# Products of constants issued ahead of twelve TensorE waits in a three-layer forward pass

## The chip, the cores and the metric

The kernel runs on one core of a Trainium2 chip. A core has TensorE (called PE in the profile; its weight loads are PEld), VectorE (DVE), ScalarE (ACT), GpSimd (POOL) and SyncE (SP), which issues most of the DMAs. The metric is the device time of one execution in microseconds. TensorE's clock has two levels, 1.2 and 2.4 GHz; the profile gives the granted share of the higher one, so 0.50 is 1.2 GHz and 1.00 is 2.4 GHz.

## The reference

All tensors are float32, the batch is 1, the sequence 256, the width 1024. A first block has two layers, a second block one:

```python
h = h + even_mixer(rms_norm(h), ...)      # differential attention + gated recurrence (RG-LRU)
h = h + swiglu(rms_norm(h), ...)          # 1024 -> 2816 -> 1024
h = h + pool_mixer(rms_norm(h), ...)      # means over windows of 2, 4, 8, 16
h = h + moe_swiglu(rms_norm(h), ...)      # 8 experts of 3584, top 2 of 8
h = rms_norm(h)
# second block, modulated by c, with 256 tokens of context
x = h + mod[2] * hybrid_mixer(...)        # gated delta rule and GLA, both directions
x = x + mod[5] * hier_moe(...)            # 4 groups of 8 experts of 512, top 2 in a group
out = rms_norm(x)
```

## The kernel before

The program is written engine by engine, each engine with its own list of instructions, and all order between engines is made by semaphores. TensorE's list is the block that begins at L655. `mm` is the matmul call, `chain` a row of calls that add up in one bank, `take(name)` a wait until a block of weights has landed in one of the six slots of the ring. PSUM is one tensor `ps` of eight banks of 512 columns. `table` holds constants: the unit matrix `ident` in columns 0 to 127, then a matrix of ones, a lower and an upper triangle up to column 511.

In order of time TensorE's list is this. The first mixer: projections, `scores`, `gates`, `weights_turned` (transposes of the attention weights, L1000), `weighted`, with the vectors of modulation `ada(0..2)` between them; the output projection; `norm_T(1)` (16 transposes of the normed rows, L693), which waits for them with `xn_ready`. The feed-forward part: 22 chunks, each with 16 gate and up products of 256 columns (L665) and four down products of 512 columns (L1071). `norm_T(2)`, the pooling products, `norm_T(3)`, the router. Then `routed_units`, 56 units of three weight blocks each (products at L782 and L797), which ends in a branch on the number of rounds (L934: the round for overflowing experts is skipped). Then the second block: keys, values and queries of the context and the sequence, the squares of keys (L1129) and of queries (`query_squares`, L1172), the delta rule in ticks (`gram`, `turn`, `product`, `step` and so on, L1219 and L1229 among them), the GLA part with two directions `d` (L1365 transposes, then the state sum, then eight levels of L1388 and L1393), the branch outputs, `norm_T(5, 6)`, the second router (L1459), and `routed_pairs`: ranks (L910), a gather, and 16 pairs of experts (L873, L893, L860).

At each place where TensorE needs something from DVE or ACT there is a `pe.wait_ge`, and the instructions behind it in the list stand still until it holds. The norm of a result is a chain of POOL, DVE and ACT steps, as is the softmax, so TensorE is idle at these places. SP issues each load of weights when the slot is free, that is when TensorE has read the block that was there before: in `routed_units` at L528, for the second block at L520, in `routed_pairs` at L616.

Of the kernel before, what the change touches and what calls it, by code (L numbers as in the profile page):

```python
# [140 lines left out]
def build(nc, ins, out):  # L141

    ctx = ExitStack()
    with ctx:
# [18 lines left out]
        def inc(name):  # L163

            if name not in shared:
                return sem(name)
            k = emitted[name] = emitted.get(name, 0) + 1
            group, value = place[name, k]
            emitted[group] = emitted.get(group, 0) + 1
            assert emitted[group] == value, (name, k)  # L170
            return sem(group)

        def at(name, value):

            if name not in shared:
                return sem(name), value
            group, total = place[name, value]
            return sem(group), total
# [7 lines left out]
        table = sb("table", [P, N_CONST])  # L186
# [8 lines left out]
        ps = ctx.enter_context(nc.psum_tensor("ps", [P, 8, 512], F32))  # L195
# [35 lines left out]
        ident = table[:, C_ID:C_ID + P]  # L231
# [421 lines left out]
        def _(pe):  # L653
            mm = nc.tensor.matmul

            def take(name):
                i = number[name]
                _, src, k, n, _ = entry(i)
                pe.wait_ge(*at("loaded%d" % (i % NSLOT), 16 * (i // NSLOT + 1)))
                return slot(i, k, n)  # L660

            def chain(outp, pairs):
# [2 lines left out]
                    last = mm(outp, l, r, start=(i == 0), stop=(i == n - 1))  # L665
                return last

            def ada(g):

                if g == 0:  # L670
                    pe.wait_ge(*at("c_silu", 1))
                    pe.wait_ge(*at("qk_copied", 2))
                else:
                    pe.wait_ge(*at("rg_sig", g))
                w = [take("ada%d" % (4 * g + j)) for j in range(4)]
                for k in range(KC):
                    for j in range(4):
                        last = mm(ps[32 * j:32 * j + 32, 5 + g % 2, :], scT[k // 4][:, k % 4, :], w[j][:, k, :],
                                  start=(k == 0), stop=(k == KC - 1))
                last.then_inc(inc("ada"), 1)  # L680
# [14 lines left out]
            def norm_T(i, x_at=None):  # L695
                for t in range(NT):
                    for c in range(KC):
                        if c % 4 == 0:
                            pe.wait_ge(*at("xn_ready", 4 * (i if x_at is None else x_at) + 2 * t + c // 4 + 1))
                        last = nc.tensor.transpose(ps[:, c // 2, (c % 2) * S + t * P:(c % 2) * S + (t + 1) * P],  # L700
                                                   xn[:, t, c * P:(c + 1) * P], ident)
                        if t == NT - 1 and c % 2:
                            last.then_inc(inc("xnT_ready"), 1)
# [201 lines left out]
                scatter(PAIRS, 0)  # L905

            def routed_pairs():
                pe.wait_ge(*at("sel2_ready", 1))
                E = E2
                mm(ps[:, 7, 0:E], tri_le, seli[:, 0, 0:E], start=True, stop=True)  # L910
                chain(ps[:, 7, E:2 * E], [(ones, seli[:, 0, 0:E]), (tri_le, seli[:, 1, 0:E])])
                chain(ps[:, 7, 2 * E:3 * E], [(ones, seli[:, 0, 0:E]), (ones, seli[:, 1, 0:E])]).then_inc(inc("rank2_sum"), 1)
                pe.wait_ge(*at("m2_zeroed", 1))
                pe.sem_inc(sem("m2_y"), 2)
                pairs_round("m", 0)
                pe.wait_ge(*at("rounds2_ready", 1))
                rounds = pe.value_load(rounds_i[1][0:1, 0:1], min_val=1, max_val=8)
                with pe.If(rounds > 1):
                    with pe.Fori(1, rounds) as r:
                        pairs_round("x", r)  # L920
# [66 lines left out]
            def gates(g):  # L987

                if g == 0:
                    pe.wait_ge(*at("xb_copied", 1))  # L990
                    pe.wait_ge(*at("xc_ready", 1))
                    pe.wait_ge(*at("wgate_in", 16 * 16))
                else:
                    pe.wait_ge(*at("gb_copied", 1))
                b = 6 - 2 * g
                for m in range(4):
                    last = mm(ps[:, b + m // 2, (m % 2) * S:(m % 2 + 1) * S], wgate[:, g, m, :], xc[:, m, :], start=True, stop=True)
                last.then_inc(inc("gates_ready"), 1)

            def weights_turned(qt):  # L1000
                pe.wait_ge(*at("w_ready", qt + 1))
                for kb in range(qt + 1):
                    for h in range(H):
                        last = nc.tensor.transpose(ps[:, kb, h * P:(h + 1) * P], wts[:, h, kb * P:(kb + 1) * P], ident)
                last.then_inc(inc("wT_ready"), 1)

            def weighted(qt):
                pe.wait_ge(*at("wT_copied", qt + 1))
                for h in range(H):
                    last = chain(ps[:, 2, h * P:(h + 1) * P],  # L1010
                                 [(wT[:, kb, h, :], vtok[:, kb, h * P:(h + 1) * P]) for kb in range(qt + 1)])
                last.then_inc(inc("o_ready"), 1)
# [26 lines left out]
            ada(1)  # L1039
            ada_cols(0)  # L1040
            gates(1)
            weights_turned(1)
            weighted(1)
            ada_cols(1)
            ada(2)
# [4 lines left out]
            for n in range(2):  # L1050
# [3 lines left out]
                    last = chain(ps[:, 4 + 2 * n + t, :], [(mixT[:, k, t * P:(t + 1) * P], w[:, k, :]) for k in range(KC)])  # L1054
                last.then_inc(inc("y_ready"), 1)

            norm_T(1)
            chunks = [(u, j) for u, (f0, n) in enumerate(FU) for j in range(n // P)]
            for n in range(len(chunks) + 1):
# [13 lines left out]
                    last.then_inc(inc("down_done"), 1)  # L1073

            norm_T(2)
            pe.wait_ge(*at("xn_ready", 16))
            pe.wait_ge(*at("hTc_ready", 1))
            pe.wait_ge(*at("hTc_act", 1))
# [25 lines left out]
            for k in range(KC):  # L1104
                piece(2, k)
                for t in range(NT):
                    last = mm(ps[:, 5, t * E1:(t + 1) * E1], hTx[:, k, t * P:(t + 1) * P], rw1[:, k, :],
                              start=(k == 0 and t == 0), stop=(k == KC - 1), skip_group_check=True)
# [2 lines left out]
            routed_units()  # L1111

            w = take("k")
            pe.wait_ge(*at("res_ready", 4))
            for m in range(4):
                chain(ps[:, 4 + m, S:2 * S], [(w[:, k, m * P:(m + 1) * P], hT[:, k, S:2 * S]) for k in range(KC)])
# [5 lines left out]
            for m in range(4):  # L1122
                chain(ps[:, m, 0:S], [(w[:, k, m * P:(m + 1) * P], hTx[:, k, :]) for k in range(KC)])\
                    .then_inc(inc("v2_proj"), 1)
                if m == 1:
                    pe.wait_ge(*at("kraw", 1))
                    pe.wait_ge(*at("k_sq", 1))
                    for h in range(H):
                        last = mm(ps[:, 4 + h, :], ones, sq[:, h, :], start=True, stop=True)  # L1129
                    last.then_inc(inc("k_ss"), 1)  # L1130
# [36 lines left out]

            def query_squares():
                pe.wait_ge(*at("vTok_ready", 1))
                pe.wait_ge(*at("q_sq", 1))  # L1170
                for i in range(2):
                    last = mm(ps[:, 4 + i, :], ones, sq[:, 2 * i:2 * i + 2, 0:S], start=True, stop=True)  # L1172
                last.then_inc(inc("q_ss"), 1)
# [5 lines left out]
            def gram(s_, d):  # L1179
                n, t = 2 * s_ + d, TILE[d][s_]  # L1180
                bx, by = banks(s_, d)
                if s_ >= 2:
                    pe.wait_ge(*at("S_ready", n - 3))
                elif s_ == 1:
                    pe.wait_ge(*at("qF_ready", 1))
                for h in range(H):
                    kf = kF[:, h, t * P:(t + 1) * P]
                    mm(bx[:, h, :], kf, kf, start=True, stop=True)
                for h in range(H):
                    last = mm(by[:, h, :], gdec[:, t, 4 * d + h:4 * d + h + 1].to_broadcast([P, P]), (tri_le, tri_ge)[d],  # L1190
                              start=True, stop=True)
                last.then_inc(inc("gram"), 1)
# [135 lines left out]
            for d in range(2):  # L1328
# [20 lines left out]
                else:  # L1349
# [8 lines left out]
                    last.then_inc(inc("gate_proj"), 1)  # L1358
                    pe.wait_ge(*at("z_silu", 2))

                pe.wait_ge(*at("kd_ready", d + 1))
                pe.wait_ge(*at("hv_ready", 1))
                for t in range(NT):
                    for h in range(H):
                        last = nc.tensor.transpose(ps[:, t, h * P:(h + 1) * P], Wd[:, h, t * P:(t + 1) * P], ident)  # L1365
                last.then_inc(inc("kdT_ready"), 1)
                pe.wait_ge(*at("kdTok_ready", d + 1))
                if d == 1:
                    pe.wait_ge(*at("gate_kept", 2))
# [5 lines left out]
                for l in range(8):  # L1375
                    b = 4 + 2 * (l % 2)
                    n = 8 * d + l
# [8 lines left out]
                    for t in range(NT):  # L1386
                        for h in range(H):
                            last = mm(ps[:, b + t, h * P:(h + 1) * P], kx[:, h, t * P:(t + 1) * P], qx[:, h, t * P:(t + 1) * P],  # L1388
                                      start=True, stop=True)
                    last.then_inc(inc("att_ready"), 1)  # L1390
                    m = l // 2
                    for k in range(4 * (l % 2), 4 * (l % 2) + 4):
                        last = mm(ps[:, m // 2, (m % 2) * S:(m % 2 + 1) * S], w[:, k, m * P:(m + 1) * P], hTx[:, k, :],  # L1393
                                  start=(k == 0), stop=(k == KC - 1))
# [4 lines left out]
                for h in range(H):  # L1399
                    last = mm(ps[:, 3, h * P:(h + 1) * P], kW2[1][:, h, kt * P:(kt + 1) * P], qW2[1][:, h, qt * P:(qt + 1) * P],  # L1400
                              start=True, stop=True)
# [48 lines left out]
                    last.then_inc(inc("grow_sum"), 1)  # L1450

            pe.wait_ge(*at("frow_ready", 1))
            norm_T(5, 6)
            pe.wait_ge(*at("res_ready", 6))
            pe.wait_ge(*at("router2_in", 64))
# [1327 lines left out]
```

## Time and profile before

| | |
|---|---|
| median of 3 runs | 2503.74 us (2502.93 to 2504.47) |
| profiled execution, span from first to last instruction | 2502.1 us |
| TensorE matmul busy | 2373.7 us, 95% of the span, 23992 instructions |
| weight loads busy | 1540.9 us, 62% |
| DVE, ACT, POOL busy | 630.1, 305.4, 157.2 us |
| mean granted clock | 0.973 |
| bytes read from HBM | 674.08 MB |

The profiled execution gives its span alone; the median of the runs is 1.6 us more. A row of the timeline merges neighbouring instructions of one line: its start, its length, the line, the shape, the number of instructions, and in brackets the idle time of the engine before it and what ended that. A stretch in a window row has each engine's busy time with its number of instructions, then the granted clock, the share of time in which the DMA engines were busy, and GB/s.

### The profile page before, as it was taken

How to read it: one execution, taken by the hardware profiler on the slowest of the kernel's cores; microseconds unless marked ns; L12 is line 12 of the kernel's file. 1: busy time of each engine (PE TensorE's matmuls, PEld its weight loads, DVE VectorE, ACT ScalarE, POOL GpSimd, SP SyncE). 2: the span in 40 equal slices, each digit the busy share in tenths (PEclk: the TensorE clock that was granted, in tenths of full speed). 3: DMA queues.
4: the chain of work that ended last, by engine and by line, in shares of the span. 5: the costliest groups of instructions: out<-in, count | busy, mean ns of one | idle time of the engine just before them, and what ended most of it. 6: DMA issues, size and time to landing. Idle time of an engine off the chain costs nothing.

```text
span 2502.1 us, 51438 instructions
## 1 busy us (share of the span) xinstructions
PE 2373.7 (95%) x23992; PEld 1540.9 (62%) x23992; DVE 630.1 (25%) x1135; ACT 305.4 (12%) x510; POOL 157.2 (6%) x173
## 2 busy tenths in 40 slices
PE   7889999999999999999999897899999899999998
PEld 5647776766666666666666777885768554444443
DVE  1640002201011101101010255741534332222223
ACT  1210001000000000000000143312333100000000
POOL 2000000000000000000000014340202000000000
PEclk9989999999999999999999988999999899999999
DMA  8783424699999999999999400022124579999996
GB/s 320 253 319 136 168 84 160 238 394 370 393 369 394 369 384 378 367 394 370 393 368 390 176 1 1 1 102 101 68 101 140 192 294 399 399 399 400 398 400 265
DMA packets 274310, 678.50 MB, mean 271 GB/s; under 512 B 5907, under 2 KB 9454, under 8 KB 269870
## 3 DMA queue, kind: packets, MB, share of 16 engines
q1 hardware_dynamic: 271664, 669.01, 71.2%
q0 software_dynamic: 2112, 6.04, 0.7%
q8 instruction: 193, 3.16, 0.5%
q14 instruction: 23, 0.19, 0.0%
q10 hardware_dynamic: 318, 0.10, 0.0%
HBM read 674.08 MB, written 1.05 MB: 270 GB/s over the span
## 4 chain that ended last, share of the span: by engine, by line
PE 74%; SPq 9%; DMA 7%; DVE 6%; ACT 1%; issue 1%; POOL 0%; DVEq 0%; POOLq 0%; ACTq 0%
PE ps L665 23%; PE ps L782 20%; PE ps L797 9%; SPq L616 8%; DMA ring<-in_moe_wd 5%; PE ps L873 4%; PE ps L1071 3%; PE ps L893 3%; DMA ring<-in_w_exp_up 2%; SPq L528 2%; PE ps L860 1%; PE ps L1219 1%; PE ps L1388 1%; PE ps L1393 1%; ACT arena L2258 1%
## 5 line engine op out<-in xcount | busy, mean ns | idle before, releaser
L782 PE MATMUL ps<-ring,arena 128*32 128x256 f32 x10752 | 590.6, 379 | 0.5 <-DVE arena L1926 0.5
L782 PEld LDWEIGHTS ps<-ring,arena 128*32 128x32 f32 x10752 | 348.6, 110 | 232.6 <-issue 2.7
L665 PE MATMUL ps<-hT,ring 128*128 128x256 f32 (+1 forms) x1680 | 401.2, 399 | 5.9 <-issue 5.9
L665 PEld LDWEIGHTS ps<-hT,ring 128*128 128x128 f32 x1680 | 321.8, 192 | 87.7 <-issue 47.9
L2258 ACT ACTIVATE arena<-ps 128x512 f32<-128x512 f32 (+5 forms) x238 | 117.0, 523 | 1747.2 <-PE ps L782 781.6
L797 PE MATMUL ps<-ring,arena 128*32 128x256 f32 x5376 | 300.5, 379 | 1.8 <-DMA ring<-in_moe_wd 1.6
L797 PEld LDWEIGHTS ps<-ring,arena 128*32 128x32 f32 x5376 | 173.9, 110 | 117.6 <-DMA ring<-in_moe_wd 3.4
L1608 DVE TENSOR_TENSOR arena<-arena,ps 128x384 f32<-128x384 f32 x56 | 31.0, 554 | 591.7 <-ACT arena L2258 591.7
L873 PE MATMUL ps<-ring,arena 128*64 128x512 f32 x672 | 152.6, 609 | 14.8 <-DMA ring<-in_w_exp_up 14.8
L665 PE MATMUL ps<-arena 128*128 128x128 f32 (+1 forms) x1032 | 128.8, 285 | 8.3 <-ACT arena L2258 3.3
L665 PEld LDWEIGHTS ps<-arena 128*128 128x128 f32 x1032 | 124.8, 201 | 13.3 <-ACT arena L2258 3.8
L2640 POOL TENSOR_SCALAR small<-small 128x1 f32<-128x1 f32 x18 | 5.9, 330 | 1948.9 <-ACT arena L2258 1948.8
L873 PEld LDWEIGHTS ps<-ring,arena 128*64 128x64 f32 x672 | 51.6, 140 | 113.7 <-issue 113.7
L893 PE MATMUL ps<-ring,arena 128*64 128x512 f32 x352 | 113.3, 595 | 0.9 <-DVE res L1677 0.9
L1612 DVE STREAM_TRANSPOSE arena<-arena 128x384 f32<-128x384 f32 x56 | 32.4, 578 | 200.7 <-PE ps L797 200.4
L1071 PE MATMUL ps<-ring,arena 128*128 128x512 f32 x176 | 79.0, 592 | 0.0
L873 PE MATMUL ps<-arena 128*64 128x512 f32 x272 | 77.5, 593 | 0.0
L2258 ACT ACTIVATE arena<-arena 128x512 f32<-128x512 f32 (+4 forms) x71 | 58.4, 861 | 119.5 <-POOL arena L2742 33.2
L665 PE MATMUL ps<-ring,arena 128*128 128x512 f32 (+2 forms) x176 | 61.0, 501 | 5.4 <-DVE arena L1481 5.4
L1704 DVE TENSOR_TENSOR table<-arena,ps 128x512 f32<-128x512 f32 x16 | 11.0, 688 | 218.9 <-PE ps L873 218.9
L893 PEld LDWEIGHTS ps<-ring,arena 128*64 128x64 f32 x352 | 34.8, 137 | 46.3 <-issue 46.3
L860 PE MATMUL ps<-arena 128*128 128x512 f32 x136 | 62.9, 605 | 0.0
(378 smaller groups left out, 1971.7 us busy)
## 6 DMA issues: line engine op xcount, KB each, us to landing
ring<-in_moe_wg SPq DMA_DIRECT2D x56, 2048.0 KB, 12.5
ring<-in_moe_wu SPq DMA_DIRECT2D x56, 2048.0 KB, 17.5
ring<-in_moe_wd SPq DMA_DIRECT2D x56, 2048.0 KB, 19.0
ring<-in_w_exp_up SPq DMA_DIRECT2D x22, 2048.0 KB, 20.0
ring<-in_w_exp_down SPq DMA_DIRECT2D x22, 2048.0 KB, 19.1
ring<-in_w_exp_gate SPq DMA_DIRECT2D x20, 2048.0 KB, 23.7
ring<-in_w_in SPq DMA_DIRECT2D x14, 2048.0 KB, 9.4
ring<-in_w_ada SPq DMA_DIRECT2D x12, 2048.0 KB, 13.8
```

The lines of the kernel that those rows point to most:

```text
L528: sp.dma_start(ring[:, s_, :].rearrange("p (k n) -> p k n", k=k), src.rearrange("(k p) n -> p k n", p=P))\
L616: sp.dma_start(dst, w[2 * p + j, :, :].rearrange(rows_, p=P)).then_inc(inc("loaded%d" % b), 16)
L665: last = mm(outp, l, r, start=(i == 0), stop=(i == n - 1))
L782: last = mm(o_, x_[:, k, 32 * r:32 * r + 32], gu[:, :, k, :, q, :], start=(k == 0), stop=(k == KC - 1))
L797: last = mm(flat[32 * q:32 * q + 32, 3 * 512 + S * r:3 * 512 + S * r + S], un_actT[:, r, c, :], d_[:, c, q * S:(q + 1) * S], start=(j == 0 ...
L860: last = mm(ps[:, (6 if t == 0 else 4) + c, :], GcT[:, 1 - b, t, :], ysb[:, c * 512:(c + 1) * 512], start=True, stop=True)
L873: last = mm(ps[64 * j:64 * j + 64, part, :], x_[:, k, 64 * j:64 * j + 64], w_[j][:, k, :], start=(k == 0), stop=(k == KC - 1))
L893: last = mm(ps[64 * j:64 * j + 64, 4 + h_, :], pr_actT[:, c, 64 * j:64 * j + 64], w_[j][:, c, h_ * 512:(h_ + 1) * 512], start=(c == 0), st ...
L1071: last = mm(ps[:, 4 + 2 * t + c, :], actb[:, (n - 1) % 4, t * P:(t + 1) * P], d_[:, j, c * 512:(c + 1) * 512], start=(n == 1), stop=(n == ...
L1608: V.tensor_tensor(un_act, un_sg, up_, ALU.mult).then_inc(inc("m1_act"), 1)
L1612: V.transpose(un_actT.rearrange("p r c s -> p (r c s)"), un_act.rearrange("p r n -> p (r n)"))\
L2258: return nc.scalar.activation(*a, **k)
```

## The change

A helper `awake(n, b)` issues `n` products of `ident` with the first 512 columns of `table` into bank `b`. Nobody reads that result: the bank is free at that point and is started anew by its next use. Twelve calls are added, with 115 products in all, in two places behind a further wait (`s_shifted` and `f_sig`) or one drawn forward (`res_ready` 2). Nothing else changes.

```diff
@@ -665,6 +665,11 @@
                     last = mm(outp, l, r, start=(i == 0), stop=(i == n - 1))
                 return last
 
+            def awake(n, b):
+
+                for _ in range(n):
+                    mm(ps[:, b, :], ident, table[:, 0:512], start=True, stop=True)
+
             def ada(g):
 
                 if g == 0:
@@ -905,6 +910,7 @@
                 scatter(PAIRS, 0)
 
             def routed_pairs():
+                awake(10, 0)
                 pe.wait_ge(*at("sel2_ready", 1))
                 E = E2
                 mm(ps[:, 7, 0:E], tri_le, seli[:, 0, 0:E], start=True, stop=True)
@@ -1039,7 +1045,10 @@
             ada(1)
             ada_cols(0)
             gates(1)
+            pe.wait_ge(*at("s_shifted", 2))
+            awake(19, 3)
             weights_turned(1)
+            awake(3, 3)
             weighted(1)
             ada_cols(1)
             ada(2)
@@ -1054,6 +1063,7 @@
                     last = chain(ps[:, 4 + 2 * n + t, :], [(mixT[:, k, t * P:(t + 1) * P], w[:, k, :]) for k in range(KC)])
                 last.then_inc(inc("y_ready"), 1)
 
+            awake(8, 0)
             norm_T(1)
             chunks = [(u, j) for u, (f0, n) in enumerate(FU) for j in range(n // P)]
             for n in range(len(chunks) + 1):
@@ -1073,6 +1083,8 @@
                     last.then_inc(inc("down_done"), 1)
 
             norm_T(2)
+            pe.wait_ge(*at("res_ready", 2))
+            awake(8, 4)
             pe.wait_ge(*at("xn_ready", 16))
             pe.wait_ge(*at("hTc_ready", 1))
             pe.wait_ge(*at("hTc_act", 1))
@@ -1111,6 +1123,7 @@
             routed_units()
 
             w = take("k")
+            awake(13, 0)
             pe.wait_ge(*at("res_ready", 4))
             for m in range(4):
                 chain(ps[:, 4 + m, S:2 * S], [(w[:, k, m * P:(m + 1) * P], hT[:, k, S:2 * S]) for k in range(KC)])
@@ -1123,6 +1136,7 @@
                 chain(ps[:, m, 0:S], [(w[:, k, m * P:(m + 1) * P], hTx[:, k, :]) for k in range(KC)])\
                     .then_inc(inc("v2_proj"), 1)
                 if m == 1:
+                    awake(11, 3)
                     pe.wait_ge(*at("kraw", 1))
                     pe.wait_ge(*at("k_sq", 1))
                     for h in range(H):
@@ -1167,6 +1181,7 @@
 
             def query_squares():
                 pe.wait_ge(*at("vTok_ready", 1))
+                awake(17, 6)
                 pe.wait_ge(*at("q_sq", 1))
                 for i in range(2):
                     last = mm(ps[:, 4 + i, :], ones, sq[:, 2 * i:2 * i + 2, 0:S], start=True, stop=True)
@@ -1182,6 +1197,8 @@
                 if s_ >= 2:
                     pe.wait_ge(*at("S_ready", n - 3))
                 elif s_ == 1:
+                    if d == 0:
+                        awake(6, 6)
                     pe.wait_ge(*at("qF_ready", 1))
                 for h in range(H):
                     kf = kF[:, h, t * P:(t + 1) * P]
@@ -1358,12 +1375,17 @@
                     last.then_inc(inc("gate_proj"), 1)
                     pe.wait_ge(*at("z_silu", 2))
 
+                if d == 0:
+                    pe.wait_ge(*at("f_sig", 1))
+                    awake(6, 4)
                 pe.wait_ge(*at("kd_ready", d + 1))
                 pe.wait_ge(*at("hv_ready", 1))
                 for t in range(NT):
                     for h in range(H):
                         last = nc.tensor.transpose(ps[:, t, h * P:(h + 1) * P], Wd[:, h, t * P:(t + 1) * P], ident)
                 last.then_inc(inc("kdT_ready"), 1)
+                if d == 1:
+                    awake(4, 7)
                 pe.wait_ge(*at("kdTok_ready", d + 1))
                 if d == 1:
                     pe.wait_ge(*at("gate_kept", 2))
@@ -1450,6 +1472,7 @@
                     last.then_inc(inc("grow_sum"), 1)
 
             pe.wait_ge(*at("frow_ready", 1))
+            awake(10, 0)
             norm_T(5, 6)
             pe.wait_ge(*at("res_ready", 6))
             pe.wait_ge(*at("router2_in", 64))
```

## Rows read from the trace of the kernel before

**Rows 1.** The page: the span of the profiled execution.

```profile
span 2502.1 us, 51438 instructions
```

**Rows 2.** The page, costliest groups: count | busy us, mean ns | idle before.

```profile
L1071 PE MATMUL ps<-ring,arena 128*128 128x512 f32 x176 | 79.0, 592 | 0.0
```

**Rows 3.** The chain that ended last, from 400 to 412 us: start, us, what.

```profile
403.44 6.88 PE ps L1071 x16
```

**Rows 4.** Timeline of PE at the twelve places: start, us, line, shape, count, idle before.

```profile
131.51 1.97 PE L1004 MATMUL ps<-table,arena 128*128 128x128 f32 x8 [8.67 <-DVE arena L1795]
134.92 3.68 PE L665 MATMUL ps<-arena 128*128 128x128 f32 x16 [1.45 <-DVE arena L1800]
...
179.20 3.60 PE L700 MATMUL ps<-table,arena 128*128 128x128 f32 x16 [3.52 <-DVE arena L1481]
...
417.44 6.87 PE L665 MATMUL ps<-ring,arena 128*128 128x256 f32 x21 [5.38 <-DVE arena L1481]
...
1404.58 15.80 PE L665 MATMUL ps<-hT,ring 128*128 128x256 f32 x64 [5.89 <-issue]
...
1448.65 5.57 PE L1129 MATMUL ps<-arena,table 128*128 128x512 f32 x8 [5.11 <-ACT arena L2258]
...
1511.60 3.75 PE L1172 MATMUL ps<-arena,table 128*128 128x512 f32 x4 [8.15 <-ACT arena L2258]
...
1524.89 2.08 PE L1188 MATMUL ps<-arena 128*128 128x128 f32 x8 [2.95 <-DVE arena L1995]
...
1531.46 1.95 PE L1229 MATMUL ps<-ring 128*128 128x128 f32 x16
...
1768.80 1.06 PE L1365 MATMUL ps<-table,arena 128*128 128x128 f32 x8 [2.74 <-DVE arena L2148]
...
1869.41 3.43 PE L665 MATMUL ps<-arena 128*128 128x128 f32 x16 [2.16 <-ACT arena L2258]
...
1985.96 3.65 PE L700 MATMUL ps<-table,arena 128*128 128x128 f32 x16 [4.35 <-DVE arena L1481]
...
2001.27 0.64 PE L910 MATMUL ps<-arena,table 128*128 128x32 f32 x2 [4.75 <-DVE arena L1527]
```

**Rows 5.** Windows behind five of the waits: PE, PEld, DVE, ACT, POOL busy, PEclk, DMA.

```profile
417.40:421.70 4.30, 4.26 (x10) 3.46 (x11) 0.45 (x1) 0.00 (x0) 0.00 (x0) 0.50 0.03 7
1448.60:1454.00 5.40, 5.35 (x8) 2.42 (x9) 0.00 (x0) 0.00 (x0) 0.00 (x0) 0.64 0.00 0
1511.60:1518.00 6.40, 6.40 (x21) 4.33 (x22) 0.21 (x1) 0.60 (x1) 0.86 (x1) 0.55 0.00 0
...
1985.90:1996.50 10.60, 10.54 (x48) 10.17 (x48) 3.10 (x7) 1.93 (x4) 2.43 (x4) 0.50 0.45 174
2001.20:2010.50 9.30, 8.28 (x44) 8.06 (x44) 5.40 (x29) 1.70 (x3) 0.00 (x0) 0.59 0.32 124
```

**Rows 6.** Timeline of DVE: what three added calls wait for, and the last ranks.

```profile
119.51 2.29 DVE L1786 TENSOR_TENSOR arena<-arena,small 128x2048 f32<-128x2048 f32 x1
...
410.35 2.48 DVE L1879 TENSOR_TENSOR res<-res,ps 128x512 f32<-128x512 f32 x4 [6.03 <-PE ps L1071]
...
1496.00 2.48 DVE L1990 COPY arena<-ps 128x512 f32<-128x512 f32 x4 [0.72 <-PE ps L1165]
...
2003.72 0.19 DVE L1535 TENSOR_REDUCE small<-ps 128x1 f32<-128x32 f32 x1 [2.17 <-PE ps L665]
...
2008.45 1.37 DVE L2246 TENSOR_SCALAR arena<-ps,small 128x128 f32<-128x128 f32 x4
```

**Rows 7.** Line L934, the branch behind the units: duration ns min/median/max, start.

```profile
L934 PEldq COMPARE_BRANCH  x1: 6295/6295/6295, 1398.1 to 1398.1; - x1
```

**Rows 8.** Windows of the units, of the start of the pairs, and of the pairs.

```profile
470.00:1390.00 920.00, 918.23 (x16596) 567.91 (x16592) 100.43 (x165) 39.65 (x78) 0.00 (x0) 1.00 1.01 379
2005.00:2017.00 12.00, 12.00 (x64) 7.62 (x65) 6.41 (x26) 1.57 (x2) 0.00 (x0) 0.84 0.00 0
2020.00:2470.00 450.00, 433.77 (x2120) 192.07 (x2116) 120.09 (x225) 23.37 (x45) 0.00 (x0) 0.99 1.04 398
```

## The prediction

> **What bounds the kernel now.** I read the span first [rows 1], then the idle gaps of TensorE along its timeline [rows 4], then the granted clock right behind these gaps [rows 5], and last the stages on either side [rows 8]. TensorE is the bound nearly everywhere: in the expert units it is busy 918.23 of 920 us with the clock at 1.00 [rows 8], so whatever comes later in front of them ends later behind them. In the pairs the DMA engines are full, at 398 GB/s [rows 8]. But between 2005 and 2017 us nothing moves at all [rows 8]: SP's next load waits for the slot that TensorE frees with its first pair, so that stream, and with it the end, moves with TensorE's arrival at the pairs. A microsecond won or lost on TensorE ahead of about 2017 us is therefore a microsecond of the total. In the twelve places TensorE idles 1.45 to 8.67 us [rows 4], and behind them it runs at the lower clock level for a while: 0.50 to 0.64 in the stretches shown [rows 5].
>
> **Price of one added product.** The tempting number is the mean of one 128x512 instruction, 592 ns, or its spacing: 16 of them in 6.88 us, 0.43 us each [rows 2, 3]. Neither is the price of a call. The feed-forward part makes 22 x 4 = 88 calls of `mm` at L1071 and the page counts 176 instructions [rows 2]: a float32 call is two passes. The four calls at L1129 likewise stand as x8 [rows 4]. So one call costs 2 x 0.43 = 0.86 us at full clock, and 115 calls 98.9 us. The waits they are to stand in sum to 55.1 us [rows 4]. The Trainium skill (TensorE: Matmul & The Clock Gate, Part 2, "Back-to-back issue gap") gives 512/2.4 + 2.5, some 216 ns, for a warm product of 512 columns; by it the 115 would be an estimated 25 us, every call would fit its wait, and the sum would be rival 1's. The trace contradicts it for this data type, with 0.43 us a pass and two passes.
>
> **Place by place.** For each: calls x 0.86, less the idle time it fills, less what the lower clock costs today behind the wait (cold instructions take twice as long). Where the added calls end after the old wait, the surplus lies bare on TensorE's path.
>
> - `weights_turned(1)`: the calls start when TensorE comes free, at 131.51 - 8.67 = 122.84, since `s_shifted` is posted at 121.80 [rows 4, 6]. 19 x 0.86 = 16.3 against 8.67: +7.7. Three more, 2.6 against the 1.45 of the copies: +1.1. Given back: 8 transposes in 1.06 for 1.97 and 16 passes in 1.95 for 3.68 [rows 4], 2.7. Sum **+6.1**.
> - `norm_T(1)`: 6.9 against 3.52, +3.4; 16 transposes then take about 2 us for 3.60 [rows 4]. **+1.8**.
> - Pooling: the calls sit behind `res_ready` 2, posted at 412.83 [rows 6], so only 4.6 us of the wait are left: +2.3. The clock row gives back 0.50 x 4.26 = 2.1 [rows 5]. **+0.2**.
> - Keys of the context: here the idle time is not a wait for data. It is marked "issue", and L934, the skip of the overflow round, takes 6.295 us from 1398.1 to 1404.4 [rows 4, 7]. `awake(13, 0)` stands behind that branch, so it starts where the keys start today, with nothing to hide in: 13 x 0.86 = 11.2, plus some 2 because its start runs at the lower level, as the keys' start does now; the keys win the same 2 back (64 passes of 256 columns in 15.80 against 64 x 0.215 = 13.8, half a 512-column pass each [rows 3, 4]). **+11.2**.
> - Squares of keys: 9.5 against 5.11, +4.4; 0.36 x 5.35 = 1.9 back [rows 5]. **+2.4**.
> - Squares of queries: `vTok_ready` is posted by 1498.48 [rows 6], before TensorE comes free at 1503.45, so 14.6 stands against the full 8.15, +6.5; 0.45 x 6.40 = 2.9 back [rows 5]. **+3.6**.
> - `gram` of the second chunk: 5.2 against 2.95, +2.2; from 1524.89 to 1531.46 run 32 passes of 128 columns, 6.6 us, which at the speed of L1229 (16 in 1.95) take 3.7 [rows 4]. **-0.7**.
> - GLA, first direction: 5.2 against 2.74, +2.4; the 16 passes of the state sum give back about 1.5, as in the second direction below. **+0.9**.
> - GLA, second direction: 3.4 against 2.16, +1.3; 16 passes in 1.95 for 3.43 [rows 4]. **-0.2**.
> - `norm_T(5, 6)`: 8.6 against 4.35, +4.3; the transposes and the router's 32 narrow passes run at 0.50 for all of 10.54 busy us [rows 5], so 5.3 come back at most; I take 5 for what waits on DVE. **-0.8**.
> - Ranks: 8.6 against 4.75, +3.9. Bounds: 0.41 x 8.28 = 3.4 would come back if TensorE set the pace [rows 5], but from 2003.72 to 2008.45 DVE works alone toward the pairs [rows 6], so only about 1.1 does: +0.5 to +2.8. If the clock falls during the router's narrow passes just ahead, the ten calls run partly at the lower level, up to 3 us more. **+4**, nearer the upper end (+6), since narrow passes hold the lower level today in this place [rows 5].
>
> The sum is 6.1 + 1.8 + 0.2 + 11.2 + 2.4 + 3.6 - 0.7 + 0.9 - 0.2 - 0.8 + 4 = 28.5 us. Against the span of 2502.1 us [rows 1] that is 2530.6; the median lies 1.6 us above the span, which gives 2532 us. Unseen: where the clock falls in the short stretches that the change doesn't touch (the first router, the small projections, the delta rule). Shifting the program can lengthen or shorten these by a microsecond or two each, up or down; I take 0 +/- 5.
>
> **The rivals.**
>
> 1. *The calls fit, and the kernel is faster.* Were a call one pass of 0.43 us, each would end inside its wait except the 13 behind the branch (+5.6). The rest gives back about 2.7 + 1.6 + 2.1 + 1.9 + 2.9 + 2.9 + 1.8 + 1.5 + 5 + 1, some 23 us: 2503.7 - 23 + 5.6 = 2486 us. For it: no row of the trace shows a product with the unit matrix as one operand and constants as the other. The x8 of L1129 and the x176 of L1071 speak against it [rows 2, 4]. The sum falls by 1.1 us for each 0.01 us of price, so it decides at about 0.61 us a call; the pass's mean of 592 ns [rows 2], taken as the price of a call, would already make the change a small gain. Chance 0.05.
> 2. *The delay ahead of the units is swallowed.* If loads set the pace there, the first three places (+8.1) cost nothing: 2524 us. For it: DMA is at 1.01 busy share and 379 GB/s. Against it: TensorE has 1.8 us of idle time in 920, and the pairs show 398 GB/s, so the stream has room [rows 8]. Chance 0.12.
> 3. *The branch hides its calls.* If TensorE could take the 13 calls while the branch runs, they would cost 11.2 - 5.9 - 2 = 3.3 for 11.2: 2524 us. The row shows the branch ending 0.2 us before the first keys, so I give it 0.06.
> 4. *The calls don't count as work.* If the clock falls during them as it does in the idle wait, the surplus of about 40 us and the 11 us behind the branch take twice as long and the 25 us given back stay lost: 28.5 + 40 + 11 + 25, some 2608 us. The Trainium skill (the same page, Part 4, "PE-mode transpose") says that transposes don't bring the clock up; the added calls have the unit matrix as an operand but are plain products. Here the dense transposes at 1985.96 run at 0.50 [rows 4, 5], which agrees without proving it. Plain 512-column passes did get the clock back at L1129 (0.64 in the mean [rows 5]). Chance 0.05.
>
> **How the numbers follow.** The forecast has 0.70, the rivals 0.28, the rest 0.02 lies near no change. What a measurement can tell from no change here is about 0.2%, 5 us. Slower by more: 0.70 + 0.12 + 0.06 + 0.05 = 0.93; faster: 0.05; the same: 0.02. The range goes from rivals 2 and 3 less the clock's 5 us, 2518 (they give 2524), to the forecast with the upper bound at the ranks and most of the clock's scatter, 2542; rivals 1 and 4 lie outside, 0.1 together.
>
> **What would show it.** Each `awake` in the new trace as twice as many MATMUL rows as calls, 230 in all, spaced 0.43 us; nearly no idle time left ahead of the twelve places, because TensorE arrives after the semaphore; the granted clock at 1.00 behind ten of them; the 26 passes behind L934 beginning only when that branch has ended, with the keys 11 to 13 us behind it; the units beginning about 8 us later and lasting as long as before; SP's first load behind 2017 us some 28 us later. The forecast is wrong if a call is one row, if the units shrink by what came before them, or if the passes of the added calls stand 0.86 us apart for long.

## The result: slower by 1.2%

The changed kernel takes 2534.85 us (median of four runs, 2529.1 to 2537.97) against 2503.84 before: a ratio of 1.0119, with a 95% interval of 1.0107 to 1.0132. The profiled execution spans 2532.4 us, 30.3 more than the one of before [rows 1]; the sum had 28.5. One of the five executions of the kernel with six calls ahead of the branch, below, took 10442.43 us at a mean granted clock of 0.225; it is in no ratio, and the median without it would be 2483.68 us.

The page of the changed kernel, its span, the granted clock in 40 slices (9 is 0.9 or more) and the group of the added calls (count | busy us, mean ns | idle before):

```profile
span 2532.4 us, 51895 instructions
...
PEclk9999999999999999999999999999999999999999
...
L671 PE MATMUL ps<-table 128*128 128x512 f32 x230 | 105.7, 616 | 6.6 <-issue 5.8
```

115 calls are 230 instructions, two passes each, as with L1071 and L1129 of before [rows 2, 4]. TensorE spends 105.7 us in them. The waits they stand in held 55.1 us, and 5.8 us of idle time ahead of them are still there, those of the branch. The clock is what the change wanted: the mean rose from 0.973 to 0.988.

Timeline of PE of the changed kernel at ten of the twelve places (start, us, line, shape, count, idle before); L671 are the added calls, and lines below them have moved by 5 to 23:

```profile
122.52 16.47 PE L671 MATMUL ps<-table 128*128 128x512 f32 x38
138.83 1.04 PE L1010 MATMUL ps<-table,arena 128*128 128x128 f32 x8
139.70 2.74 PE L671 MATMUL ps<-table 128*128 128x512 f32 x6
142.28 1.95 PE L665 MATMUL ps<-arena 128*128 128x128 f32 x16
...
181.46 7.03 PE L671 MATMUL ps<-table 128*128 128x512 f32 x16
188.32 1.91 PE L705 MATMUL ps<-table,arena 128*128 128x128 f32 x16
...
420.74 7.13 PE L671 MATMUL ps<-table 128*128 128x512 f32 x16 [0.82 <-DVE res L1902]
427.71 13.98 PE L665 MATMUL ps<-ring,arena 128*128 128x256 f32 x64
...
1412.80 14.48 PE L671 MATMUL ps<-table 128*128 128x512 f32 x26 [5.78 <-issue]
1427.12 13.98 PE L665 MATMUL ps<-hT,ring 128*128 128x256 f32 x64
...
1464.10 9.61 PE L671 MATMUL ps<-table 128*128 128x512 f32 x22
1473.54 3.60 PE L1143 MATMUL ps<-arena,table 128*128 128x512 f32 x8
...
1527.76 14.76 PE L671 MATMUL ps<-table 128*128 128x512 f32 x34
1542.36 1.88 PE L1187 MATMUL ps<-arena,table 128*128 128x512 f32 x4
...
1793.35 5.31 PE L671 MATMUL ps<-table 128*128 128x512 f32 x12
1798.49 1.04 PE L1385 MATMUL ps<-table,arena 128*128 128x128 f32 x8
1800.71 2.05 PE L665 MATMUL ps<-arena 128*128 128x128 f32 x16 [1.18 <-ACT arena L2281]
...
2008.04 8.75 PE L671 MATMUL ps<-table 128*128 128x512 f32 x20
2016.62 1.91 PE L705 MATMUL ps<-table,arena 128*128 128x128 f32 x16
2019.06 3.73 PE L1482 MATMUL ps<-arena,hT 128*128 128x36 f32 x32 [0.53 <-DVE hT L1527]
2022.63 10.53 PE L671 MATMUL ps<-table 128*128 128x512 f32 x20
2032.99 0.30 PE L916 MATMUL ps<-arena,table 128*128 128x32 f32 x2
```

Read it beside [rows 4]. The idle times in brackets that stood there are gone or short, but for the branch's: TensorE now comes to nearly every place later than what it waits for. What follows each block runs at full clock: 8 transposes in 1.04 for 1.97 us, 16 passes in 1.95 for 3.68, the eight passes of the squares of keys in 3.60 for 5.57, the router's 32 narrow passes in 3.73 for 7.01, by this row of before:

```profile
1989.51 7.01 PE L1459 MATMUL ps<-arena,hT 128*128 128x36 f32 x32
```

So both halves of the mechanism are there, the calls that outlast their waits and the clock that comes back, and the first is the larger one.

Windows of the changed kernel: the calls behind the branch, the norm and router near the end, the calls at the ranks, the units, the pairs (PE, PEld, DVE, ACT, POOL busy, PEclk, DMA share, GB/s):

```profile
1412.80:1427.20 14.40, 14.40 (x27) 6.22 (x28) 3.36 (x6) 2.30 (x4) 3.01 (x5) 0.79 0.11 39
...
2016.70:2023.00 6.30, 5.77 (x50) 5.46 (x49) 2.07 (x5) 1.93 (x4) 0.00 (x0) 1.00 0.22 82
2022.60:2033.10 10.50, 10.50 (x24) 4.59 (x23) 4.27 (x23) 0.20 (x1) 0.00 (x0) 0.84 0.59 200
470.00:1398.00 928.00, 925.51 (x16724) 571.91 (x16728) 101.91 (x169) 40.11 (x80) 0.00 (x0) 1.00 1.00 375
2050.00:2470.00 420.00, 403.93 (x1983) 179.12 (x1981) 111.98 (x210) 22.08 (x42) 0.00 (x0) 0.99 1.04 398
```

In the units TensorE is as busy as before [rows 8], and the pairs take their loads at the same 398 GB/s [rows 8]: nothing was swallowed. SP's first load behind the standstill comes 29.9 us later, and the end moves by 30.3 (timeline of SP, before and after):

```profile
2017.71 0.37 SPq L616 DMA_DIRECT2D arena<-in_w_exp_up  x1
```

```profile
2047.63 0.37 SPq L616 DMA_DIRECT2D arena<-in_w_exp_up  x1
```

### The profile page after: what moved, and what is told of

The parts are those of the page before. It is cut to its first block, busy times and chain, and to the rows that moved or that the text cites. A ratio compares the mean times of both kernels' runs of the same rounds, so it can differ in the third digit from the quotient of the medians.

```text
span 2532.4 us, 51895 instructions
## 1 busy us (share of the span) xinstructions
PE 2449.7 (97%) x24222; PEld 1565.2 (62%) x24222; DVE 630.9 (25%) x1135; ACT 305.3 (12%) x510; POOL 156.8 (6%) x173
## 4 chain that ended last, share of the span: by engine, by line
PE 77%; SPq 11%; DMA 7%; DVE 4%; issue 1%; ACT 1%; POOL 0%; POOLq 0%; DVEq 0%; ACTq 0%
PE ps L665 23%; PE ps L787 20%; SPq L616 9%; PE ps L802 9%; DMA ring<-in_moe_wd 5%; PE ps L671 4%; PE ps L878 4%; PE ps L1081 3%; PE ps L898 2%; PE ps L1236 2%; SPq L528 1%; PE ps L865 1%; PE ps L1410 1%; PE ps L1415 1%; PE ps L765 1%
## 5 line engine op out<-in xcount | busy, mean ns | idle before, releaser
L878 PE MATMUL ps<-ring,arena 128*64 128x512 f32 x672 | 150.9, 603 | 12.4 <-DMA ring<-in_w_exp_up 12.4
L665 PE MATMUL ps<-arena 128*128 128x128 f32 (+1 forms) x1032 | 121.9, 276 | 4.7 <-DVE arena L2208 1.7
L665 PEld LDWEIGHTS ps<-arena 128*128 128x128 f32 x1032 | 118.3, 192 | 9.9 <-issue 4.2
L671 PE MATMUL ps<-table 128*128 128x512 f32 x230 | 105.7, 616 | 6.6 <-issue 5.8
L671 PEld LDWEIGHTS ps<-table 128*128 128x128 f32 x230 | 44.8, 197 | 61.1 <-issue 60.0
```

Source lines behind the costliest of these rows:

```text
L671: mm(ps[:, b, :], ident, table[:, 0:512], start=True, stop=True)
L878: last = mm(ps[64 * j:64 * j + 64, part, :], x_[:, k, 64 * j:64 * j + 64], w_[j][:, k, :], start=(k == 0), stop=(k == KC - 1))
```

## The experiments

Each time below is compared with that of the kernel before on the same chip. The edit shown is made to the changed kernel, or, where the expectation says "as the run with", to the kernel of that run; "..." stands for lines left out.

**Half the calls.** Each count such that count x 0.86 fits the wait, none behind the branch.

```diff
-            awake(19, 3)
+            awake(9, 3)
...
-            awake(13, 0)
+            pass
```

> The same places with about half the calls (9 and 1, 4, 5, 5, 9, 3, 3, 2, 5, 5 instead of 19 and 3, 8, 8, 11, 17, 6, 6, 4, 10, 10), and none behind the branch: 51 calls for 115. Theory (a call is two passes, 0.86 us, and the change is slow only because its calls outlast the waits): each call now ends inside its wait, TensorE resumes when it did before, and what the lower clock cost comes back: 2.7 + 1.6 + 2.1 + 1.9 + 2.9 + 2.9 + 1.5 + 1.5 + 3 + 1, some 21 us less than before, 2483 us, not under 2478 nor over 2492. Rival (the calls themselves disturb, or the places lie off the path): within 5 us of 2504, or slower.

Measured: 2487.18 us, ratio 0.9934 (0.9921 to 0.9948). The loss becomes a gain of 16.8 us by leaving out calls. The timeline of PE shows the calls inside their waits at most places, with some idle time left, here at `weights_turned(1)` and the squares of queries; the last row is the ranks (start, us, line, shape, count, idle before):

```profile
122.46 7.89 PE L671 MATMUL ps<-table 128*128 128x512 f32 x18
131.29 1.09 PE L1010 MATMUL ps<-table,arena 128*128 128x128 f32 x8 [0.94 <-DVE arena L1818]
...
1498.53 7.89 PE L671 MATMUL ps<-table 128*128 128x512 f32 x18
1506.76 1.98 PE L1187 MATMUL ps<-arena,table 128*128 128x512 f32 x4 [0.34 <-ACT arena L2281]
...
1977.93 6.24 PE L671 MATMUL ps<-table 128*128 128x512 f32 x10
```

The transposes start at 131.29 as they did at 131.51 [rows 4], and take 1.09 us for 1.97. The gain is 4 us under the 21 expected. Places differ from the list in both directions. In the profile, 1.2 us were given back between `weights_turned` and the output projection: TensorE arrives there early and waits longer for the modulation on VectorE (1.4 us where it had been 0.5). Another 1.0 us went into the keys behind the branch, which ran at the lower clock for longer than before (16.79 us for 15.80 [rows 4]), and 1.8 us were lost in the pairs behind 2200 us, where TensorE waits for loads. `norm_T(1)` gave 0.7 for 1.6, the small projections behind the squares of keys lost 1.7, and the ranks gave 0.6 for 1: there the clock fell, so five calls took 6.1 us and outlasted the wait of 4.75. On the other side the first router gained 1.7, the GLA's first direction 1.1 more than listed, and `norm_T(5, 6)` with its router 0.8 more. Why the stretches without calls shifted is not shown. The keys of this kernel:

```profile
1399.12 16.79 PE L665 MATMUL ps<-hT,ring 128*128 128x256 f32 x64 [5.88 <-issue]
```

**Only the calls behind the branch, 13 and 26.**

```diff
-            awake(19, 3)
+            pass
...
-            awake(13, 0)
+            awake(26, 0)
```

All the other calls are taken out like the first; the second pair of lines stands in the second kernel alone.

> Only the 13 calls behind the branch are kept. Theory (they start when the branch ends and stand bare): 11.2 us more than before, 12.4 if the first of them run at the lower clock for longer, so 2515 to 2517 us. Rival (the branch hides part of them): 3.3 us more, 2507.

> As the run with the 13 calls behind the branch, but 26 of them. Theory (0.86 us a call at full clock): 11.2 us over that run. Rival (0.43 us a call): 5.6 us over it. Lower clock throughout: 22 us.

Measured: 2514.32 us, ratio 1.0041 (1.0025 to 1.0056), and 2525.65 us, ratio 1.0090 (1.0074 to 1.0105). The first is 10.4 us over before, 0.7 under the range expected and far from the 3.3 of a branch that hides them; 13 more add 11.3 us, 0.87 us a call. That is the price of a call, measured without any wait around it, from medians whose runs scatter over 4 us each; 0.43 us a call would have been 5.6. The timelines of PE with 13 and with 26 (columns as above):

```profile
1407.14 13.92 PE L671 MATMUL ps<-table 128*128 128x512 f32 x26 [5.69 <-issue]
```

```profile
1406.72 24.11 PE L671 MATMUL ps<-table 128*128 128x512 f32 x52 [5.69 <-issue]
1430.67 13.98 PE L665 MATMUL ps<-hT,ring 128*128 128x256 f32 x64
```

The same 5.7 us of idle time stand ahead of the calls, whether 13 or 26: calls issued behind the branch don't use it. In these two executions the 13 more take 10.2 us and not 11.2, since up to the next row the 13 took 2.6 us more than 13 x 0.86, with a granted clock of 0.82, and the 26 only 1.6 more than 26 x 0.86, with 0.94.

**All calls but those behind the branch.**

```diff
-            awake(13, 0)
+            pass
```

> The change as it is, without the 13 calls behind the branch. Theory (at the other places the calls outlast the waits by some 40 us and give 25 back): 17 to 19 us over before, 2521 to 2523 us. Rival (only the calls behind the branch cost, the rest fits and gains): under 2504 us.

Measured: 2522.35 us, ratio 1.0072 (1.0056 to 1.0087), 17.7 us over before. So the loss isn't the branch's alone: at the other eleven places the surplus outweighs what the clock gives back, by what the sum had said (28.5 - 11.2 = 17.3).

**Six calls ahead of the branch.**

```diff
                 units_round("m", 0)
+                awake(6, 0)
                 pe.wait_ge(*at("rounds1_ready", 1))
```

> As the run with half the calls, and six calls more at the end of the units' list, ahead of the wait for the number of rounds and of the branch at its end. Theory (TensorE's list runs ahead of the engine, so calls issued before the branch run while it is fetched): the 5.2 us of calls lie inside the 5.9 us of idle time, the keys run at full clock from their start, 1.8 us less than that run, about 2485.4 us. Rival (the branch begins only when the calls have ended): 3 to 5 us more than that run, 2490 to 2492 us.

Measured: 2483.76 us, ratio 0.9921 (0.9906 to 0.9936), 3.4 us under the run with half the calls in the medians, where 1.8 was expected. The two intervals overlap and this kernel's runs spread from 2482.37 to 2487.95 us, so that the calls run under the branch is shown by the trace and not by the time. The timeline of PE and the branch's row (line, engine, operation: duration ns min/median/max, first and last start us):

```profile
1393.10 5.42 PE L671 MATMUL ps<-table 128*128 128x512 f32 x12
...
1399.60 14.05 PE L665 MATMUL ps<-hT,ring 128*128 128x256 f32 x64 [1.08 <-issue]
```

```profile
L941 PEldq COMPARE_BRANCH  x1: 6271/6271/6271, 1393.2 to 1393.2; - x1
```

The branch begins at 1393.2, just when the first call starts on the engine, and the calls run under it: here the sequencer doesn't wait for products that it has already issued. The keys stand 0.5 us later against the units than in the run with half the calls, but run at full clock, 14.05 us for 16.79: 2.2 us net of the 3.1 between the two profiled spans.

**Transposes in place of products.**

```diff
-                    mm(ps[:, b, :], ident, table[:, 0:512], start=True, stop=True)
+                    [nc.tensor.transpose(ps[:, b, 0:P], table[:, 0:P], ident) for _ in range(8)]
```

> As the run with half the calls, but each call is eight transposes of a 128x128 block of constants, one pass of 0.107 us each, so the same time on TensorE. If what keeps the clock is any full stream of instructions: the same time as that run, some 2483 us, with the granted clock at 1.00 behind the waits. If transposes don't count as work, as the Trainium skill says (TensorE: Matmul & The Clock Gate, Part 4): the clock is at 0.50 behind the waits as before, some transposes run at the lower level and outlast their wait, and the time is 2504 to 2520 us.

Measured: 2484.89 us, ratio 0.9928 (0.9913 to 0.9943), the same as half the calls within the scatter. Two of its windows, one over the squares of keys and one over those of queries (columns as above):

```profile
1438.00:1450.00 12.00, 11.25 (x65) 8.69 (x64) 3.56 (x7) 5.81 (x4) 0.00 (x0) 1.00 0.00 0
1496.00:1506.60 10.60, 10.60 (x97) 10.36 (x95) 10.49 (x18) 4.42 (x5) 5.03 (x5) 1.00 0.01 2
```

The clock stays at 1.00 while TensorE does nothing but transposes for 8 us. It even came up under them: at the ranks it had fallen, as in the run with half the calls, when the 40 transposes began, and it rose while TensorE ran nothing else (their row, then two windows inside it):

```profile
1977.96 6.23 PE L671 MATMUL ps<-table 128*128 128x128 f32 x40
```

```profile
1978.10:1981.40 3.30, 3.30 (x18) 3.30 (x17) 2.79 (x15) 0.00 (x0) 0.00 (x0) 0.50 0.57 124
1981.50:1984.00 2.50, 2.50 (x25) 2.50 (x24) 1.39 (x9) 0.20 (x1) 0.00 (x0) 1.00 1.02 387
```

The Trainium skill (TensorE: Matmul & The Clock Gate, Part 4, "PE-mode transpose") says that transposes don't count as work for the clock; for these float32 transposes of full blocks the measurement says otherwise, and it decides.

**Two calls among narrow passes.**

```diff
             for t in range(4):
+                if t == 2:
+                    awake(2, 7)
                 last = chain(ps[:, 6, t * 16:(t + 1) * 16],
```

> As the run with six calls ahead of the branch, and two calls of 0.86 us more in the middle of the 64 passes of 16 columns behind the squares of keys, where the clock falls though TensorE is never idle. Theory (narrow passes don't hold the clock, and two full calls would): 1.7 us of calls against some 4 us of lower clock, 2 us less than that run. Rival (two calls don't change where the clock falls): 1.7 us more.

Measured: 2487.68 us (2481.84 to 2491.98), ratio 0.9935 (0.9921 to 0.9948): inconclusive as a time, the scatter is larger than either effect. The profiles of the run without and with the two calls do tell something (windows, columns as above; the first is without, and the second has the row of the calls):

```profile
1452.00:1467.00 15.00, 15.00 (x87) 14.68 (x86) 10.06 (x15) 4.84 (x5) 0.00 (x0) 0.66 0.00 1
```

```profile
1456.08 3.48 PE L671 MATMUL ps<-table 128*128 128x512 f32 x4
...
1452.00:1467.00 15.00, 15.00 (x91) 12.91 (x90) 10.07 (x15) 4.83 (x5) 0.00 (x0) 0.77 0.00 1
```

TensorE is busy for all 15 us in both, yet the clock fell to 0.66 in the mean while it ran passes of 16 columns back to back. With the two calls it is 0.77, but the calls themselves ran mostly at the lower level: they took 3.3 us and not 1.7. From the start of these passes to that of the projection behind them the stretch is 13.95 us with them and 13.55 without. That is neither the 2 us won of the theory nor the 1.7 us lost of the rival: they pay for themselves at best.

**Three calls in the last pair.**

```diff
+                        if x == "m" and p == PAIRS - 1 and part == 1:
+                            pe.wait_ge(*at("m2_gcT", R * G_ + p + 1))
+                            awake(3, 7)
                         w_ = [weights(p, part, j, KC) for j in range(2)]
```

> As the run with six calls ahead of the branch, and three calls of 0.86 us more in the last pair of experts, in the 2.8 us in which TensorE waits for the second block of weights. Theory (behind the last load TensorE alone sets the end, and there the lower clock costs 1.7 us in that run's profile): 1 to 2 us less than that run, 2482 us. Rival (the loads set the end, the clock in the pairs costs nothing): the same as that run, 2483.8 us.

Measured: 2483.06 us, ratio 0.9919 (0.9905 to 0.9932), 0.7 us under the run with the six calls. Timeline of PE around the last wait for loads, first without, then with the three calls (columns as above):

```profile
2448.97 8.78 PE L878 MATMUL ps<-ring,arena 128*64 128x512 f32 x32 [2.76 <-DMA ring<-in_w_exp_up]
```

```profile
2444.99 2.84 PE L671 MATMUL ps<-table 128*128 128x512 f32 x6
2448.23 7.09 PE L881 MATMUL ps<-ring,arena 128*64 128x512 f32 x32 [0.40 <-DMA ring<-in_w_exp_up]
```

In the profiles the 32 passes behind the last load take 7.09 for 8.78 us, so the theory holds there; in the medians 0.7 us can't be told from nothing. This kernel and the one with six calls ahead of the branch are the fastest measured, some 21 us under the kernel before.

## Why the prediction was right

Measured step by step as the difference of a place's shift in the two timelines, start after minus start before, ahead of the place and behind it:

| place | predicted | measured |
|---|---|---|
| `weights_turned(1)`, `weighted(1)` | +6.1 | +6.1 |
| `norm_T(1)` | +1.8 | +1.9 |
| pooling | +0.2 | +0.2 |
| keys, behind the branch | +11.2 | +12.4 |
| squares of keys | +2.4 | +2.2 |
| squares of queries | +3.6 | +3.4 |
| `gram` | -0.7 | -0.9 |
| GLA, first direction | +0.9 | -0.5 |
| GLA, second direction | -0.2 | -0.4 |
| `norm_T(5, 6)` and router | -0.8 | -0.5 |
| ranks | +4 | +3.8 |
| stretches not touched | 0 +/- 5 | +2.7 |

- *The price.* 0.86 us a call, from counting instructions against calls. The run with 26 calls measured it alone, 0.87. Rival 1 is out. The 216 ns that the prediction quotes from the Trainium skill (TensorE: Matmul & The Clock Gate, Part 2, "Back-to-back issue gap") don't hold for these float32 products: a pass takes 0.43 us and a call is two.
- *The branch.* The calls behind it stand bare, as the row of L934 said [rows 7]; rival 3 is out by the runs with 13 and 26 calls. The term was 1.2 us too small: the lower clock cost the calls 3 us (0.79 over their 14.4 us) and not the 2 assumed.
- *Carrying through.* The 8.1 us forecast from ahead of the units are 8.1 at their start and 8.3 at their end; rival 2 is out.
- *The clock.* Behind the calls it is at 1.00 everywhere, by the lengths of the rows; during them it is at 1.00 at all places but two, the branch (0.79) and the ranks (0.84). At the ranks it fell just after the router's narrow passes and the ten calls took 10.4 us for 8.6, from their start to that of the next row. Rival 4 is out; that transposes in their place wouldn't hold the clock is out too, by that run.
- *Ranks.* The sum of +4 came true with both its parts off. The lower level cost 1.8 us, of up to 3 that were allowed. And 1.8 came back, not 1.1: DVE doesn't work alone from 2003.72 to 2008.45. TensorE ran 32 passes of 128 columns in 5.87 us from 2004.56 on, which take 3.84 in the changed kernel.
- *GLA, first direction.* Mis-sized by 1.4 us: I counted only the state sum's 16 passes as given back. They came back with 1.7, and the first level's passes at L1388 behind them, 2.98 us before and 1.95 now, gave another 1.0 (timeline of PE, before and after):

```profile
1774.60 2.98 PE L1388 MATMUL ps<-arena 128*128 128x128 f32 x16
```

```profile
1802.59 1.95 PE L1410 MATMUL ps<-arena 128*128 128x128 f32 x16
```

- *Luck.* The branch's 1.2 us too little and the GLA's 1.4 too much cancel, so the total is nearer than its terms. In the step for `gram`, 32 passes at 16 in 1.95 us are 3.9 and not 3.7, which would have made it -0.5; measured were 3.6 us from their start to the next row, and -0.9. And 13 calls of 216 ns behind the branch are 2.8 us, not the 5.6 of rival 1, so the sum by that figure is not quite that rival's.
- *What wasn't counted.* 1.6 us in the small projections and transposes behind the squares of keys, 0.5 in the delta rule, 0.2 to 0.4 in the units and the pairs: the clock fell there for longer or at another moment than before. It's within the 5 us that were set aside, with no cause shown. The changed kernel also scatters more, over 8.9 us where the one before had 1.5. That goes with the clock: the shortest of its four executions has a mean granted clock of 0.989, the longest 0.986, by an estimate 28 and 36 us lost to the lower level. In which stretch it falls can't be told from one profile.

## What to carry to other kernels

Before filling a wait, price the filler by what the trace shows of the same instruction: count its instructions against its calls, take their spacing and not their mean, and multiply. A filler that outlasts its wait costs its whole surplus on the critical engine, and that can be more than the spell at the lower clock that it saves: here 115 calls lost 31 us, and 51 of them, in the same places but the branch, gained 17. The idle time of "issue" ahead of the branch was filled only by calls that were issued ahead of it.

## What the runs showed of the hardware that I had not expected

- Transposes alone kept the clock at 1.00, over 8 us of nothing else, and brought it up from 0.50 at the ranks (the run with transposes).
- The clock fell while TensorE was busy throughout, with passes of 16 columns and transposes behind them: 0.66 over 15 us (the run with six calls ahead of the branch).
- TensorE's branch over the skipped round takes 6.17 to 6.31 us in the ten profiles, and products issued ahead of it run under it.
